# Where the split weight slabs of a routed mixture-of-experts loop lie in the chip's memory, and when its row numbers and its scatter are computed

## The reference, cut to what matters

```
def swiglu(h, wg, wu, wd):
    return (jax.nn.silu(h @ wg) * (h @ wu)) @ wd

def moe_swiglu(h, router, wg, wu, wd):
    probs = jax.nn.softmax((h @ router).astype(jnp.float32), axis=-1)
    top_p, top_i = lax.top_k(probs, TOP_K)            # TOP_K = 2, 8 experts
    top_p = top_p / jnp.sum(top_p, axis=-1, keepdims=True)
    combine = jnp.sum(jax.nn.one_hot(top_i, N_EXPERTS) * top_p[..., None], axis=-2)
    out = jnp.zeros(h.shape, h.dtype)
    for e in range(N_EXPERTS):
        out = out + combine[..., e:e + 1] * swiglu(h, wg[e], wu[e], wd[e])
    return out
```

## Time and profile before

| | us |
|---|---|
| time, median of 3 runs | 1674.59 |
| lowest and highest of the 3 runs | 1671.56, 1675.25 |
| time of the profiled execution | 1668.94 |
| span of the profiled execution | 1667.0 |
| in the span: from the first unit's gather to the tenth unit's | 1105.60 to 1596.55 |
| in the span: the last of the ten down products ends, about | 1649.3 |

### The profile page before, as it was taken

One profiled execution on the slowest core, in us unless ns is written; L12 is line 12 of the kernel. 1 busy time (PEld: TensorE's weight loads), 2 busy tenths in 40 slices (PEclk: granted clock), 3 DMA queues, 4 the chain that ended last, 5 costly groups with the idle time before them and its releaser, 6 DMA issues.

```text
span 1667.0 us, 21420 instructions
## 1 busy us (share of the span) xinstructions
PE 1542.4 (93%) x7995; PEld 1262.3 (76%) x7995; DVE 1003.5 (60%) x1304; ACT 747.3 (45%) x896; POOL 184.3 (11%) x270
## 2 busy tenths in 40 slices
PE   5999999797999999899999997979999999999996
PEld 4875677666998898688567775768887888788875
DVE  3692653444342434359365434367988898888986
ACT  3423333433332333242243343146676667666763
POOL 2351200000000000314220000100000000000001
PEclk9999999998999999899999999869999999999998
DMA  6735354374333333343645329269999999999993
GB/s 225 250 109 189 130 164 152 146 271 156 111 119 120 130 100 110 127 144 125 195 152 173 134 76 353 102 234 332 316 323 320 332 329 329 325 335 335 317 329 124
DMA packets 176576, 347.72 MB, mean 209 GB/s; under 512 B 7114, under 2 KB 48348, under 8 KB 176240
## 3 DMA queue, kind: packets, MB, share of 16 engines
q1 hardware_dynamic: 162224, 316.17, 55.4%
q0 software_dynamic: 5936, 19.92, 3.5%
q10 hardware_dynamic: 8352, 10.75, 1.8%
HBM read 335.20 MB, written 13.48 MB: 209 GB/s over the span
## 4 chain that ended last, share of the span: by engine, by line
PE 59%; issue 22%; DMA 8%; DVE 6%; ACT 3%; POOL 2%; POOLq 0%; SPq 0%; DVEq 0%; ACTq 0%
PE bank L1151 14%; PE bank L1153 14%; PE bank L1152 14%; PE bank L1113 5%; DMA arena<-h_rows,row_of_slot 4%; PE bank L1077 4%; PE bank L1528 2%; DMA ring<-in_cache_mem_k 1%; POOL counts L2609 1%; DMA out_new_mem_k_prompt<-arena 1%; DVE arena L2325 1%; ACT arena L1719 1%; PE bank L1580 1%; PE bank L1649 1%; DVE arena_parts L808 1%
## 5 line engine op out<-in xcount | busy, mean ns | idle before, releaser
L808 DVE TENSOR_TENSOR arena_parts<-ring,arena_parts 128x2048 fp32r<-128x2048 f32 (+1 forms) x156 | 331.3, 2142 | 176.9 <-ACT arena_parts L803 176.9
L1151 PE MATMUL bank<-arena_parts,features_parts 128*128 128x512 f32 (+2 forms) x1056 | 410.5, 389 | 13.1 <-DVE ring_low_parts L967 7.3
L1153 PE MATMUL bank<-arena_parts 128*128 128x512 f32 (+1 forms) x928 | 363.1, 391 | 0.0
L803 ACT ACTIVATE arena_parts<-ring 128x2048 fp32r<-128x2048 f32 (+1 forms) x156 | 277.4, 1796 | 148.3 <-PE bank L1153 132.9
L1152 PE MATMUL bank<-arena_parts 128*128 128x512 f32 (+1 forms) x704 | 258.9, 368 | 0.0
L1152 PE MATMUL bank<-arena_parts,features_parts 128*128 128x512 f32 (+1 forms) x672 | 257.4, 383 | 0.0
L1151 PEld LDWEIGHTS bank<-arena_parts,features_parts 128*128 128x128 f32 x1056 | 201.3, 191 | 51.9 <-issue 11.1
L1153 PEld LDWEIGHTS bank<-arena_parts 128*128 128x128 f32 x928 | 176.2, 190 | 40.1
L1719 ACT ACTIVATE arena<-bank 128x512 f32<-128x512 f32 (+3 forms) x160 | 85.3, 568 | 228.9 <-PE bank L1153 138.4
L1153 PE MATMUL bank<-arena_parts,features_parts 128*128 128x512 f32 (+1 forms) x480 | 182.0, 379 | 0.0
L1152 PE MATMUL bank<-ring_low_parts,features_parts 128*128 128x512 f32 (+1 forms) x384 | 146.6, 382 | 0.0
(11 more groups left out here) (288 smaller groups left out, 1913.0 us busy)
## 6 DMA issues: line engine op xcount, KB each, us to landing
ring<-in_moe_w_up SPq DMA_DIRECT2D x40, 1024.0 KB, 6.2
ring<-in_moe_w_down SPq DMA_DIRECT2D x30, 1024.0 KB, 5.2
ring<-in_w_in SPq DMA_DIRECT2D x20, 1024.0 KB, 7.4
ring<-in_moe_w_gate SPq DMA_DIRECT2D x20, 1024.0 KB, 7.4
mem_kv<-in_moe_w_gate SPq DMA_DIRECT2D x20, 1024.0 KB, 9.1
ring<-in_cache_mem_k SPq DMA_DIRECT2D x16, 1024.0 KB, 7.4
ring<-in_cache_mem_v SPq DMA_DIRECT2D x16, 1024.0 KB, 8.0
ring<-in_moe_w_gate SPq DMA_DIRECT2D x20, 768.0 KB, 5.7
```

The costliest lines, as they stand in the source:

```text
L803: nc.scalar.activation(self.part(s, 0), self.raw(s), ACT.Copy).then_inc(self.high, 1)
L808: nc.vector.tensor_tensor(self.part(s, 1), self.raw(s), self.part(s, 0).bitcast(F32), ALU.subtract).then_inc(self.split["v"], 1)
L1151: nc.tensor.matmul(out, left[0], right[0], start=start, stop=False)
L1153: return nc.tensor.matmul(out, left[1], right[0], start=False, stop=stop)
```

## The change

- Places: the slab's low part is written over the raw slab itself, as a DVE operation whose output lies where its first input lay. So a slab needs one raw place and one high place. There are now nine raw places (four in `ring`, two in `mem_kv`, three in `arena`) and six high places in `arena`. 18 is a multiple of both. A raw place is now held until PE is done with the slab, and SP waits for that (`wait_filled` on the slab nine before) and no longer for the split of the slab six before. The arena region is the 18432 floats from its end (nine places) where it was 16384 (eight places). ACT may write a high part when PE is done with the slab six before.
- Row numbers: PE computes `row` ahead of the `aT` 2 transposes, after the first of the down slabs; before, it came after the second. DVE reads it after S13 and ahead of `aT` 2 and S14; before, it came after S15.
- Scatter: half c = 0 stays between gather and the first gate product; half c = 1 goes behind the gate product of chunk 0.
- Orders: DVE and ACT do S0 and S1 ahead of the two gather results, and the result of `down` 1 after them; before, DVE did S0, `down` 1, the gathers, and then S1 and S2, and ACT did S2, S0, `down` 1, the gathers.
- In the first unit, where there is no earlier `down` 1, ACT makes a one-column copy that keeps the count of paired results even.
- The final tokens (`ytok`) move with the arena region.

```diff
@@ routed_jobs
     jobs = [(("gather", 0), (6,), "v"), (("gather", 1), (7,), "v")]
-    jobs += [(("scatter", c, t), (SCATTER_BANK[c, t],), "v") for c in range(2) for t in range(NT)]
+    jobs += [(("scatter", 0, t), (SCATTER_BANK[0, t],), "v") for t in range(NT)]
...
+            if (c, kind) == (0, "gate"):
+                jobs += [(("scatter", 1, t), (SCATTER_BANK[1, t],), "v") for t in range(NT)]
...
-    jobs += [(("down", 0, 0), (), None), (("aT", 2), (7,), "v"), (("down", 0, 1), (), None), (("row",), (6,), "v"), (("down", 0), (4,), "v"),
+    jobs += [(("down", 0, 0), (), None), (("row",), (6,), "v"), (("aT", 2), (7,), "v"), (("down", 0, 1), (), None), (("down", 0), (4,), "v"),
@@ routed_events
-    scalar = (S(ACT_FIRST, 0) + job("down", 1) + job("gather", 0) + job("gather", 1) + S(1, 5 - ACT_FIRST) + S(4, 5)
-              + job("gate", 0) + S(6) + job("ST") + S(7, 8) + job("gate", 1) + S(9, 10) + job("aT", 0) + S(11, 12)
+    scalar = (S(0, 1) + job("gather", 0) + job("gather", 1) + job("down", 1) + S(2, 3, 4)
+              + job("gate", 0) + S(5, 6) + job("ST") + S(7, 8) + job("gate", 1) + S(9, 10) + job("aT", 0) + S(11, 12)
               + job("gate", 2) + S(13, 14) + job("aT", 1) + S(15) + job("aT", 2) + S(16) + job("down", 0) + S(17))
-    vector = (S(0) + job("down", 1) + job("gather", 0) + job("gather", 1) + S(1, 2) + add((0, 0)) + S(3) + add((0, 1))
+    vector = (S(0, 1) + job("gather", 0) + job("gather", 1) + job("down", 1) + S(2) + add((0, 0)) + S(3) + add((0, 1))
               + S(4) + add((0, 2)) + S(5) + job("up", 0) + S(6) + add((1, 0)) + S(7) + add((1, 1), (1, 2)) + S(8, 9)
               + job("up", 1) + job("aT", 0) + S(10, 11, 12) + job("S") + job("up", 2) + job("aT", 1) + S(13)
-              + job("aT", 2) + S(14, 15) + job("row") + S(16) + job("down", 0) + S(17))
+              + job("row") + job("aT", 2) + S(14, 15, 16) + job("down", 0) + S(17))
@@ Loop.part
+                if self.highs:
+                    return (self.lows[s % len(self.slots)] if low else self.highs[s % self.n_parts])[:, 0:nk * w]
@@ Loop.stream
-                    if was < self.n_split:
+                    if was < self.n_split and not self.highs:
                         self.wait_split(sp, i, was, back=int(s < n_))
                     else:
                         self.wait_filled(sp, i, *self.slabs[was][5], back=int(s < n_))
@@ the loop's places
-        routed = Loop("routed", routed_jobs(), routed_slabs(), NE, ring_slots + kv_slots, ("gather", "aT", "down"),
-                      len(routed_slabs()), (), events=routed_events(), n_parts=ROUTED_PARTS, by_pool=BY_POOL)
+        at_ = (arena_w - 9 * SLAB) // 8 * 8
+        own_slots = [slice(at_ + k * SLAB, at_ + (k + 1) * SLAB) for k in range(9)]
+        routed = Loop("routed", routed_jobs(), routed_slabs(), NE, ring_slots + kv_slots + [arena[:, q] for q in own_slots[0:3]],
+                      ("gather", "aT", "down"), len(routed_slabs()), (), events=routed_events(), by_pool=BY_POOL,
+                      lows=[ring_r[:, k * SLAB:(k + 1) * SLAB] for k in range(R)]
+                      + [mem_kv_r[:, k * SLAB:(k + 1) * SLAB] for k in range(2)] + [arena_r[:, q] for q in own_slots[0:3]],
+                      highs=[arena_r[:, q] for q in own_slots[3:9]])
@@ PE, routed_step
                 if not first:
-                    for c in range(2):
-                        L.wait_emptied(pe, i, "down", c, back=1)
-                        for t in range(NT):
-                            scatter(L.begin(pe, i, "scatter", c, t), c, t).then_inc(L.filled, 1)
+                    scatter_half(0)
...
+                            if last and not first:
+                                scatter_half(1)
...
                         if (c, g) == (0, 1):
-                            turn_acts(2)
-                        if (c, g) == (0, 2):
                             pe.wait_ge(s_S, i + 2)
                             row_numbers(L.begin(pe, i, "row")).then_inc(L.filled, 1)
+                            turn_acts(2)
@@ ACT, routed_step
-                    elif key[0] == "down" and not (key[1] and first):
+                    elif key[0] == "down" and key[1] and first:
+                        A(full[:, 1:2], minus_half[:, 0:1], ACT.Copy).then_inc(L.high_out, 1)
+                    elif key[0] == "down":
```

More of the change, by code:

```diff
@@ L344, in dense_slabs @@
     return out
-ROUTED_PARTS = 4
 SCATTER_BANK = {(0, 0): 2, (0, 1): 1, (0, 2): 3, (1, 0): 4, (1, 1): 5, (1, 2): 6}
 BY_POOL = ()
-ACT_FIRST = 2
 def routed_jobs():
     jobs = [(("gather", 0), (6,), "v"), (("gather", 1), (7,), "v")]
-    jobs += [(("scatter", c, t), (SCATTER_BANK[c, t],), "v") for c in range(2) for t in range(NT)]
+    jobs += [(("scatter", 0, t), (SCATTER_BANK[0, t],), "v") for t in range(NT)]
     for c in range(3):
@@ L439, in hybrid_encoder @@
         mem_kv = sb("mem_kv", 4 * D)
+        mem_kv_at = nc.sbuf_base - 4 * 4 * D
         mv = mem_kv[:, 0:2 * D].rearrange("p (t d) -> p t d", t=2)
@@ L536, in hybrid_encoder @@
         features_r = nc.alloc_sbuf_tensor_at("features_parts", [P, KC * TOK], F32R, offset=features_at)
+        mem_kv_r = nc.alloc_sbuf_tensor_at("mem_kv_low_parts", [P, 4 * D], F32R, offset=mem_kv_at)
         ring_r = nc.alloc_sbuf_tensor_at("ring_low_parts", [P, R * SLAB], F32R, offset=ring_at)
@@ L692, in __init__ @@
             def __init__(self, name, jobs, slabs, n, slots, paired, n_split, head, after={}, events=None,
-                         n_parts=NSPLIT, by_pool=()):
+                         n_parts=NSPLIT, by_pool=(), lows=None, highs=None):
                 self.jobs, self.slabs, self.n, self.slots = jobs, slabs, n, slots
-                self.n_split, self.n_parts = n_split, n_parts
+                self.n_split, self.lows, self.highs = n_split, lows, highs
+                self.n_parts = len(highs) if highs else n_parts
                 self.parts_at = (arena_w - n_parts * 2 * SLAB) // 8 * 8
@@ L726, in __init__ @@
                 self.pairs = [key for key in (events[0] if events else [key for key, _, who in jobs if who]) if key[0] in paired]
-                if events:
-                    self.pairs = self.pairs[1:] + self.pairs[:1]
                 self.events, at = [], 0
@@ L818, in high_part, with low_part @@
                 nc.scalar.activation(out, in_, ACT.Copy).then_inc(self.high_out, 1)
-            def low_part(self, dve, i, out, in_, high, *key, back=0):
-                dve.wait_ge(self.high_out, i * len(self.pairs) + (self.pairs.index(key) + 1 - back * len(self.pairs)))
+            def low_part(self, dve, i, out, in_, high, *key):
+                dve.wait_ge(self.high_out, i * len(self.pairs) + (self.pairs.index(key) + 1))
                 self.emptied_by(nc.vector.tensor_tensor(out, in_, high.bitcast(F32), ALU.subtract), *key)
@@ L851, in hybrid_encoder @@
                         (0, 0, 0))
-        routed = Loop("routed", routed_jobs(), routed_slabs(), NE, ring_slots + kv_slots, ("gather", "aT", "down"),
-                      len(routed_slabs()), (), events=routed_events(), n_parts=ROUTED_PARTS, by_pool=BY_POOL)
+        at_ = (arena_w - 9 * SLAB) // 8 * 8
+        assert at_ >= f.at
+        own_slots = [slice(at_ + k * SLAB, at_ + (k + 1) * SLAB) for k in range(9)]
[4 more added lines that the diff above has]
+                      highs=[arena_r[:, q] for q in own_slots[3:9]])
         def units(eng, step):
@@ L976, in hybrid_encoder @@
         LAST_BANK = {(0, 0): 0, (0, 1): 1, (1, 0): 2, (1, 1): 3, (2, 0): 4, (2, 1): 6}
-        ytok = cut(arena[:, routed.parts_at:routed.parts_at + NT * D], t=NT)
+        ytok = cut(arena[:, at_:at_ + NT * D], t=NT)
         def tokens(n):
@@ L1221, in routed_step, with group @@
                 at_ = [0]
-                def group(kind, c, left, g, groups, w):
+                def group(kind, c, left, g, groups, w, done=1):
                     wt = L.slab(pe, i, at_[0])
@@ L1232, in group @@
                         ins = matmul3(out, [q[:, k, :] for q in left], [q[:, k - k0, :] for q in wt], start, stop)
-                    ins.then_inc(L.filled, 1)
+                    ins.then_inc(L.filled, done)
                 def turn_acts(c):
@@ L1247, in routed_step, with scatter_half @@
                         ins = turn(b[:, j * P:(j + 1) * P], rows_e[:, k * P:(k + 1) * P])
-                    ins.then_inc(L.filled, 1 + (2 * NT if first and g else 0))
+                    ins.then_inc(L.filled, 1 + (NT if first and g else 0))
+                def scatter_half(c):
+                    L.wait_emptied(pe, i, "down", c, back=1)
+                    for t in range(NT):
+                        scatter(L.begin(pe, i, "scatter", c, t), c, t).then_inc(L.filled, 1)
                 if not first:
-                    for c in range(2):
-                        L.wait_emptied(pe, i, "down", c, back=1)
-                        for t in range(NT):
```

(9 more changed lines are left out.)

## The result

The changed kernel takes 1655.93 us (median of 4 runs, 1653.03 to 1658.09) where the kernel before, with the runs made beside it, takes 1673.07: a ratio of 0.9902, 95% interval 0.9878 to 0.9927. The forecast was 0.94% faster, 1658.8 against 1674.59. The profiled execution took 1654.63 us, its span 1652.7.

What follows compares the result with a forecast made beforehand. It took the loop as bound by PE plus two waits, for rows and for S13; -13.0, -5.0 and +2.2 gave -15.8 us, so 1674.59 became 1658.8, range 1653 to 1668 (8 in 10), forecast chance 0.70.

Steps and rivals of the forecast that it cites:

- The bound: Changed loop: PE plus two waits per unit, 1.45 us at the gather and 0.49 at S13; without both, 52.45 us.
- Row numbers in S13's gap: PE's six small matmuls (0.58 us) move into the wait before S13's product; 0.50 us a unit, 5.0 in ten.
- The rows: Rows fetched by the indirect DMA arrive 2.2 us before the gather; nine gather waits of 1.45 us go, 13.0 gained.
- the 13.0 and the 5.0 us: Gains forecast from nine gather waits removed and from ten units' row-number matmuls falling into the wait before S13's product.
- worth nothing by itself: Six high places: no gain of their own, but they allow S0 and S1 to be done before the gather.
- The DMA rate: Loop's slab loads: 17.84 MB in 52.45 us needs 340 GB/s, from 328; bounds 328 and 369; nothing charged.
- The rival of a stuck rate: DMA stays at 328 GB/s, units at 54.4 us, waits move to the splits; 1676.8 us, chance 0.08.
- The lead of eight products: SP's slab request to use: 23 us, less 9.1 landing and two splits, leaves 9 us; cost nothing.
- The end of the unit: DVE's chain up to gather 0: low part there at 1324.9, PE wants it at 1325.2; 0.3 us spare, cost 0.
- the rival of DVE's pace: DVE's chain from S13 to gather 0 takes 1.3 us more; PE waits 1 us at nine gathers; 1667.8, chance 0.13.
- The first unit: S1 now stands between S0 and gather 0 on DVE, so the first gate product starts later: 2.2 us lost.
- The sum: Nine gathers -13.0, ten rows -5.0, first unit +2.2: -15.8 us, 0.94% faster.

Runs made afterwards that it cites:

- the run with the late S14: The changed kernel with one more DVE operation (128x1024, unused result) ahead of S14 in every unit; one run, 1664.44 us.
- the run above: The changed kernel with one more DVE operation (128x1024, unused result) ahead of gather 0 in every unit; one run, 1664.87 us.

## Why the prediction was right, point by point

- **The bound.** A unit without both waits was put at 52.45 us, and the gain at 1.95 a unit. It is 52.42 and 1.97, with PE busy throughout.
- **Row numbers in S13's gap.** Right: PE starts S13's product 0.40 us behind the first transpose of `aT` 2, which itself starts 0.59 behind the row numbers' matmuls, so these fill the wait. That S14 has nothing to spare is shown by the run with the late S14.
- **The rows.** They were to arrive 2.2 us ahead of the gather. The indirect DMA is issued at 1360.42 and lands within 7.8 us (the longest of this execution), so by 1368.2, 4.8 us ahead. 2 of that come from the marker: 2165 to 2170 ns in all ten units before, 190 to 195 after. The place of the row numbers in the order decides it, not the places of the slabs: the run with the row numbers alone has 190 to 195 ns with the old places, and the run with them put back 2.16 to 2.17 us with the new ones. This agrees with what the Trainium skill says on the page "SBUF — State Buffer", section "SBUF: two separate sides", about DVE and GpSimd excluding each other.
- **Which part earns it.** Here the working was right in the sum and loose in the shares. It booked the 13.0 and the 5.0 us to the row numbers and held the places to be "worth nothing by itself". The runs say otherwise: the row numbers alone gain nothing, and the places and orders alone 0.8 us a unit in the trace. The old kernel held a second bound, S2's request, S2 ahead of S0 on ACT, S0 and `down` 1, nearly as long as the first. The old places are only one part of it: with S0 ahead of S2 on ACT the row numbers give 1.0 of the 1.97 us without new places.
- **The DMA rate.** 340 GB/s were forecast and are measured, over 419 us. The rival of a stuck rate falls. The mean stays below the Trainium skill's figure of 358 GB/s ("DMA: Bandwidth & Descriptors", "Specifications"), and no run here shows that figure as a limit: cut into stretches of 10.75 us, the same loop moves from 236 to 396 GB/s.
- **The lead of eight products** was to leave 9 us. With three products less (8.7 us) a little should still have been left; ACT waits for loads instead, and the time grows by 8 us. So less than 8.7 us were to spare. Which term of that working was too small is not shown.
- **The end of the unit** "fits by 0.3 us": mis-sized. From the working the time between the end of DVE's operation and PE's start is missing, about 0.2 us (in the run above the split of 0.69 us starts at 1381.34 and PE at 1382.25); 0.07 are left. It cost nothing, but the rival of DVE's pace was closer than its working said.
- **The first unit** was to lose 2.2. PE's first product does start 2.17 later behind its gather (1112.70 - 1107.92 = 4.78, before 1108.21 - 1105.60 = 2.61). The unit is 55.42, and 55.84 less its gather wait (1.18 + 0.16) and 0.50 would be 54.00: a loss of 1.4. Most of the 0.8 between them is the clock: nine matmuls last over 0.6 us here, before it was twelve. That count is luck as far as the runs show, and no effect of the change: it lies between 7 and 14 in the five profiles of this study whose first product waits 0.65 to 0.74 us, and between 7 and 13 in the eight where it waits 2.8 to 4.0. The lateness of 2.2 was right.

```profile
1112.70 0.80 PE L1160 MATMUL bank<-arena_parts,features_parts 128*128 128x512 f32 x1 [2.81 <-DVE features_parts L825]
...
1116.28 0.62 PE L1162 MATMUL bank<-arena_parts,features_parts 128*128 128x512 f32 x1
1116.70 0.42 PE L1160 MATMUL bank<-arena_parts,features_parts 128*128 128x512 f32 x1
```

- **The sum.** -15.8 were forecast, -16.6 measured in the loop and behind it; 0.7 of the 0.8 between them lies in the first unit. The rest of the difference between the spans is the stretch ahead of the loop.

## What to carry to other kernels

When a wait is removed, look for the one that ends just behind it: follow each operand of the next job back to its request, and ask by how much it was early. Reordering and buffer places are then one change, and their shares can't be added up from runs of one part. A number of buffers that divides the number of slabs in a loop's turn keeps the distance between uses the same at the turn's end; with four places for 18 slabs the first two followed too closely on the last two, and no time average showed that. Six places also are two more than four; no run here tells the one reason from the other, as none has five.

## What the runs showed of the hardware that was not expected

A short idle time of PE can cost more than itself. With four high places PE stands idle 2.9 to 3.0 us in each unit, and in every second unit the clock falls afterwards, to a mean of 0.71 in the 6 us that follow (both of its levels, 1.2 and 2.4 GHz, are in that stretch):

```profile
1223.08:1278.69 55.61, 52.67 (x251) 43.76 (x250) 47.56 (x39) 36.63 (x30) 1.15 (x2) 1.00 0.91 317
1278.69:1335.91 57.22, 54.22 (x251) 44.91 (x250) 47.66 (x39) 36.63 (x30) 1.15 (x2) 0.97 0.90 315
...
1284.10:1290.00 5.90, 5.89 (x19) 4.69 (x20) 5.90 (x5) 3.23 (x2) 0.00 (x0) 0.71 0.32 98
```

That is the 1.6 us by which these units are longer (2.8 in the first of them); the idle time is the same in both kinds. This is one execution of one kernel, and why it is every second unit is open. At the start of the first unit nothing like a rule shows: how many matmuls run at the lower clock there differs from 7 to 14 between executions, whether PE stood idle for 0.7 us just before or for 3.

A one-column operation of POOL takes 2.17 or 0.19 us, by what DVE does at that moment.
